# Separate slots and groups of 6, 6 and 4 K-tiles in the first stage, and norms in halves of 1024 columns, in a two-block transformer kernel

## The reference, cut to what matters

```python
mod = c_act @ w_ada[l] + b_ada[l]
sh_m, sc_m, gt_m, sh_f, sc_f, gt_f = jnp.split(mod[:, None, :], N_MOD, axis=-1)
h = rmsnorm(x, pre_mix_norm[l]) * (1.0 + sc_m) + sh_m
proj = h @ w_in[l]
...
y = jnp.concatenate([o_hg, o_gdn], axis=-1) @ w_out[l]
x = x + gt_m * rmsnorm(y, post_mix_norm[l])
h = rmsnorm(x, pre_ffn_norm[l]) * (1.0 + sc_f) + sh_f
y = jnp.square(jax.nn.relu(h @ w_ff1[l])) @ w_ff2[l]
x = x + gt_f * rmsnorm(y, post_ffn_norm[l])
```

## Time and profile before

| | |
|---|---|
| median of 3 runs | 3014.21 us (3013.37 to 3015.81) |
| the profiled execution | 3014.85 us, its span 3013.1 us |
| PE busy | 2709.6 us, 90% of the span |
| weight loads of PE (overlapping) | 2199.4 us, 73% |
| DVE, ACT, POOL busy | 1822.8 us (60%), 1225.0 us (41%), 64.0 us (2%) |
| read from HBM | 556.28 MB, 186 GB/s over the span |

### The profile page before, as it was taken

The page is one execution under the profiler, slowest core; times in us unless marked ns, Lnnn a source line. Parts: engine busy times, 40 slices in busy tenths (PEclk is TensorE's granted clock), DMA queues, the critical chain, the costliest instruction groups (busy, mean ns, idle before and its releaser), DMA issues.

```text
span 3013.1 us, 32417 instructions
## 1 busy us (share of the span) xinstructions
PE 2709.6 (90%) x12554; PEld 2199.4 (73%) x12554; DVE 1822.8 (60%) x2185; ACT 1225.0 (41%) x1523; POOL 64.0 (2%) x90
## 2 busy tenths in 40 slices
PE   4799997587889999999988999998989999999985
PEld 2368885586668888888866877776768888788874
DVE  7669776765675555555674456667455555646454
ACT  2033444442444443444434444443544434444342
POOL 1000000000000000000001000000000000000000
PEclk8899999898989999999999999998999999999998
DMA  9977994034655555555663534444445556555451
GB/s 343 300 204 262 332 324 157 28 138 163 219 196 196 182 192 183 184 192 188 219 249 130 192 123 140 151 144 162 144 143 180 195 175 201 167 196 180 152 171 69
DMA packets 154463, 562.29 MB, mean 187 GB/s; under 512 B 9704, under 2 KB 18023, under 8 KB 150256
## 3 DMA queue, kind: packets, MB, share of 16 engines
q1 hardware_dynamic: 149968, 540.05, 52.8%
q0 software_dynamic: 4208, 20.32, 1.9%
q10 hardware_dynamic: 176, 0.40, 0.0%
HBM read 556.28 MB, written 4.46 MB: 186 GB/s over the span
## 4 chain that ended last, share of the span: by engine, by line
PE 69%; DVE 14%; issue 9%; ACT 5%; DMA 2%; POOL 1%; DVEq 0%; ACTq 0%; SPq 0%; POOLq 0%
PE banks L405 21%; PE banks L407 20%; PE banks L406 20%; ACT weights_high L352 3%; PE banks L640 2%; DVE weights_low L363 2%; PE banks L463 1%; DMA raw_weights<-in_w_in 1%; DVE x_rows L448 1%; DMA raw_weights<-in_w_ada 1%; DVE modulation L2296 1%; DVE mod_in L726 1%; DVE proj L1030 1%; DVE lhs_low L476 1%; POOL small L550 1%
## 5 line engine op out<-in xcount | busy, mean ns | idle before, releaser
L363 DVE TENSOR_TENSOR weights_low<-raw_weights,weights_high 128x1024 fp32r<-128x1024 f32 (+2 forms) x846 | 991.0, 1179 | 934.9 <-ACT weights_high L352 931.4
L352 ACT ACTIVATE weights_high<-raw_weights 128x1024 fp32r<-128x1024 f32 (+2 forms) x846 | 858.8, 1021 | 1026.9 <-PE banks L407 976.6
L405 PE MATMUL banks<-weights_high,lhs_high 128*128 128x512 f32 (+1 forms) x2208 | 875.9, 397 | 34.3 <-DVE weights_low L363 18.4
L407 PE MATMUL banks<-weights_high,lhs_low 128*128 128x512 f32 (+1 forms) x2208 | 860.2, 390 | 0.0
L406 PE MATMUL banks<-weights_low,lhs_high 128*128 128x512 f32 (+1 forms) x2208 | 859.7, 389 | 0.0
L405 PEld LDWEIGHTS banks<-weights_high,lhs_high 128*128 128x128 f32 x2208 | 416.7, 189 | 128.3 <-DVE weights_low L363 19.8
L407 PEld LDWEIGHTS banks<-weights_high,lhs_low 128*128 128x128 f32 x2208 | 416.6, 189 | 86.5
L406 PEld LDWEIGHTS banks<-weights_low,lhs_high 128*128 128x128 f32 x2208 | 417.2, 189 | 79.3 <-issue 0.2
L405 PE MATMUL banks<-weights_high,hid_high 128*128 128x512 f32 x856 | 336.6, 393 | 19.1 <-DVE hid_low L2273 9.8
L407 PE MATMUL banks<-weights_high,hid_low 128*128 128x512 f32 x856 | 334.9, 391 | 0.0
L406 PE MATMUL banks<-weights_low,hid_high 128*128 128x512 f32 x856 | 334.7, 391 | 0.0
(11 more groups left out here) (392 smaller groups left out, 2112.3 us busy)
## 6 DMA issues: line engine op xcount, KB each, us to landing
raw_weights<-in_w_ff SPq DMA_DIRECT2D x128, 1024.0 KB, 5.0
raw_weights<-in_w_in SPq DMA_DIRECT2D x96, 1024.0 KB, 5.5
raw_weights<-in_w_ada SPq DMA_DIRECT2D x84, 1024.0 KB, 5.7
raw_weights<-in_w_up SPq DMA_DIRECT2D x80, 1024.0 KB, 4.9
raw_weights<-in_w_down SPq DMA_DIRECT2D x42, 1024.0 KB, 5.1
raw_weights<-in_w_out SPq DMA_DIRECT2D x32, 1024.0 KB, 5.0
raw_weights<-in_w_ada SPq DMA_DIRECT2D x16, 768.0 KB, 6.3
raw_weights<-in_w_in SPq DMA_DIRECT2D x16, 768.0 KB, 6.9
```

What stands on the lines that cost most here:

```text
L352: act.activation(WHI[:, u % SPN, 0:c.width], RAW[:, n % RAWN, k % 2, 0:c.width], ACT.Copy).then_inc(S("high_made"), 1)
L363: dve.tensor_tensor(WLO[:, u % SPN, 0:c.width], RAW[:, n % RAWN, k % 2, 0:c.width], WHI[:, u % SPN, 0:c.width].bitcast(F32), ALU.subtract) ...
L405: nc.tensor.matmul(o, x, hi, start=(k == 0), stop=False)
L407: mm = nc.tensor.matmul(o, y, hi, start=False, stop=(k == c.kn - 1))
```

## The change

It has five parts.

- **First stage.** The K-tiles of `w_in` get four slots of their own (`FIRST_W`, laid over `weights_high` and `weights_low`), with waits of their own (`first_in`, `first_used`). The groups are 6, 6 and 4. A table (`FIRST_AFTER`) says behind which `w_ada` load SP issues each K-tile. The rows `x` are loaded after the second load rather than the sixth. POOL's loads of masks and small rows follow the second group of gates rather than the third.
- **Norms in halves.** `norm_ffn1`, `norm_in2` and `norm_ffn2` are built by one function (`norm_steps`). Columns 0 to 1023 are normed, transposed and split ahead of unit 0; columns 1024 to 2047 are normed by DVE behind unit 3, and transposed by PE ahead of unit 4. Square sums are taken in pieces, those of a chunk's first half while the next chunk runs, and one mean and power serves both row tiles where that can be.
- **Modulation rows made ahead.** The sum of row 2 stands inside the `w_out` product (ahead of unit 11 of its first chunk), that of row 3 in the last `w_ff2` chunk (ahead of unit 1), both in banks 4 to 7. The `w_out` result is taken out by a new kind of step, "post": ACT squares the bank, DVE multiplies it by the gate row. The last loads of `w_ada` stand earlier, four of them after each pair of units of the second `w_ff1` chunk, and none in the last `w_ff2` chunk.
- **Waits of the transposed rows.** PE no longer waits for the last subtraction before unit 0, but ahead of each second unit for the pair of K-tiles that it uses (`tile_waits`); so also for `mix1`, `norm_mem` and `norm_cross`.
- **The end.** The last norm is written in four pieces, each stored by SP as 512 KB, in place of two stores of 1 MB by POOL. In the `w_in_2` product the narrow product stands six units later, and the distance rows three a unit rather than two.

```diff
+        (FIRST_W,) = region(("first_weights", [128, 4, 2 * UW], F32))
-        GROUPS = [(0, 6), (6, 4), (10, 4), (14, 2)]
+        GROUPS = [(0, 6), (6, 6), (12, 4)]
+        FIRST_AFTER = {MODS[0][13]: [0], MODS[0][15]: [1], MODS[2][3]: [10], MODS[2][5]: [11, 12], MODS[2][7]: [13, 14, 15]}
+        for k in range(8):
+            FIRST_AFTER[MODS[1][2 * k + 1]] = [k + 2]
...
+                for k in FIRST_AFTER.get(x, []):
+                    if k >= 4:
+                        sp.wait_ge(S("first_used"), k - 3)
+                    sp.dma_start(first_tile(k), a["w_in"][128 * k:128 * k + 128, 4 * UW:4 * UW + FIRST_COLS]).then_inc(
+                        S(f"first_in{k % 4}"), 16)
...
+            for b, t, h, w, count, (sem, value), col in out_banks(c, i, ("post",)):
+                dve.wait_ge(sem, value)
+                dve.wait_ge(S("squares_summed"), SQUARES_BEFORE["post_mix"] + b + 4 * (col // UW) + 1)
+                dve.tensor_tensor(Y[:, t, col + 512 * h:col + 512 * h + w], PS[:, b, 0:w],
+                                  MOD[:, 0, col + 512 * h:col + 512 * h + w], ALU.mult).then_inc(S(f"bank_free{b}"), 1)
...
+            def wait(k):
+                def f(pe):
+                    pe.wait_ge(S("round_free"), round_of[name] + k // 2 + 1)
+                return f
...
+            fns = [wait(k) if k % 2 == 0 else None for k in range(KT)]
...
+        def dve_residual(dve, link, name, rows):
+
+            dve_rstd_joint(dve, link, name)
+            for t in range(TT):
+                for h in range(2):
+                    cs = slice(UW * h, UW * h + UW)
+                    dve.scalar_tensor_tensor(out=X[:, t, cs], in0=rows[:, t, cs], scalar=rstd(name, t), in1=X[:, t, cs],
+                                             op0=ALU.mult, op1=ALU.add).then_inc(S("rows_ready"), 1)
...
+            def dve_first(dve):
+                link = Chain(dve)
+                residual(dve, link)
+                dve_norm_half(dve, link, NORM_OF[name], 0, w, shift)
+                dve_split(dve, name, LH2, LL2, 8)
+
+            def dve_half(dve):
+                dve_norm_half(dve, Chain(dve), NORM_OF[name], 1, w, shift)
+
+            def dve_second(dve):
+                dve_split(dve, name, LH2, LL2, 8, first=8)
...
+            return dict(pe=tile_waits(name, (0, pe_first), (4, pe_second)), act=[act_first, None, None, None, act_second],
+                        dve=[dve_first, dve_half, None, None, dve_second])
...
+        def sp_end(sp):
+            for n in range(4):
+                t, h = divmod(n, 2)
+                sp.wait_ge(S("h_ready"), 11 + n)
+                sp.dma_start(out[128 * t:128 * t + 128, UW * h:UW * h + UW], Y[:, t, UW * h:UW * h + UW]).then_inc(
+                    S("out_written"), 16)
```

More of the change, by code:

```diff
@@ L746, in dve_first @@
             dve.wait_ge(S("columns_ready"), 1)
-            dve.wait_ge(S("cond_ready"), 1)
-            mods = [[x for x in FIRST_LOADS if x[0] == "mod" and x[1] == q] for q in range(4)]
-            for n, x in enumerate(mods[0]):
+            dve.wait_ge(S("start_mapped"), 1)
+            for n, x in enumerate(MODS[0]):
                 sums(x)
@@ L1144, in pe_mix1 @@
             mm.then_inc(S("gdn_out"), 1)
-            pe_split(pe, "mix1", P, ready=(S("mix1_ready"), 1))
+            pe_split(pe, "mix1", P, ready=(S("mix1_ready"), 1), wait=False)
         def act_mix1(act):
@@ L1456, in pool_norm_ffn1, with pe_mod_sum @@
             pool_rstd(pool, "pre_ffn")
-        def act_norm_ffn1(act):
-            act_squares(act, "post_mix", Y)
-            act_squares(act, "pre_ffn", X)
-            act_split(act, "norm_ffn1", LH2)
-        def pe_mod_sum(pe, name, row, steps):
+        def pe_mod_sum(pe, row, steps):
             pe.wait_ge(S("ada_used"), steps)
             for b in range(4):
-                pe.wait_ge(S(f"bank_free{b}"), AT[name]["done"][b])
-                mm = nc.tensor.matmul(PS[:, b, :], ONES, MOD[:, row, 512 * b:512 * b + 512], start=True, stop=True)
+                mm = nc.tensor.matmul(PS[:, 4 + b, :], ONES, MOD[:, row, 512 * b:512 * b + 512], start=True, stop=True)
@@ L1469, in pe_mod_sum, with norm_steps, pe_first, pe_second @@
             mm.then_inc(S("mod_summed"), 1)
-        def pe_norm_ffn1(pe):
-            pe_mod_sum(pe, "norm_ffn1", 2, ADA_IN + KT)
-            pe_split(pe, "norm_ffn1", Y, ready=(S("h_ready"), 2))
-        def dve_norm_ffn1(dve):
-            link = Chain(dve)
-            for b in range(4):
-                dve.wait_ge(S(f"bank_free{b}"), AT["norm_ffn1"]["done"][b])
-            dve_rows_ready(dve)
+        def norm_steps(name, squares, residual, w, shift=None, more=()):
+            h0 = H_BEFORE[name]
+            def pe_first(pe):
+                pe_split(pe, name, Y, 8, ready=(S("h_ready"), h0 + 1), wait=False)
+            def pe_second(pe):
+                pe_split(pe, name, Y, 8, ready=(S("h_ready"), h0 + 2), first=8, wait=False)
+            def act_first(act):
+                squares(act)
+                act_split(act, name, LH2, 8)
+            def act_second(act):
+                act_split(act, name, LH2, 8, first=8)
+            def dve_first(dve):
[7 more added lines that the diff above has]
+                dve_split(dve, name, LH2, LL2, 8, first=8)
+                for f in more:
+                    f(dve)
+            return dict(pe=tile_waits(name, (0, pe_first), (4, pe_second)), act=[act_first, None, None, None, act_second],
+                        dve=[dve_first, dve_half, None, None, dve_second])
@@ L1480, in dve_norm_ffn1, with pe_mod2, dve_mod2 @@
+        H_BEFORE = dict(norm_ffn1=0, norm_in2=2, norm_ffn2=8)
+        NORM_OF = dict(norm_ffn1="pre_ffn", norm_in2="mix_in", norm_ffn2="ffn2_in")
+        def pe_mod2(pe):
+            pe_mod_sum(pe, 2, ADA_IN + KT)
+        def dve_mod2(dve):
             dve.wait_ge(S("vecs_in"), 32)
-            dve.wait_ge(S("x2_in"), 16)
             dve.tensor_tensor(MOD[:, 0, :], MOD[:, 0, :], VEC[:, :], ALU.mult)
             dve.wait_ge(S("mod_summed"), 3)
-            link(dve.scalar_tensor_tensor(out=MOD[:, 2, :], in0=bank_cols(0, 4), scalar=1.0, in1=VEC2, op0=ALU.add,
-                                          op1=ALU.mult))
@@ L2092, in pe_norm_mem @@
         def pe_norm_mem(pe):
-            pe_split(pe, "norm_mem", MEMR, ready=(S("h_ready"), 6))
+            pe_split(pe, "norm_mem", MEMR, ready=(S("h_ready"), 6), wait=False)
         def dve_norm_mem(dve):
@@ L2106, in pe_norm_cross @@
         def pe_norm_cross(pe):
-            pe_split(pe, "norm_cross", Y, ready=(S("h_ready"), 8))
+            pe_split(pe, "norm_cross", Y, ready=(S("h_ready"), 8), wait=False)
         def dve_norm_cross(dve):
@@ L2409, in _ @@
             stream(sp_chunk, sp)
+            sp_end(sp)
         @block.scalar
```

337 lines of the change are left out of this document (198 added, 139 removed).

## The result

The changed kernel takes 2971.15 us (median of 4 runs, 2969.34 to 2973.16). In the same session the kernel before took 3015.01 us. The ratio is 0.9853 with a 95% interval of 0.9838 to 0.9867: faster by 43.9 us, where 29 less were forecast (2986). The forecast was right in its sign and too small in its size. The profiled execution took 2972.81 us, 42.0 less than that of before.

What follows compares the result with a forecast made beforehand. PE was taken as the bound, so only its pauses and the end could be won: -7.5 - 4.8 - 11.3 - 7.8 - 3.3 - 3.4 + 9.1 = -29.0 from 3014.85, forecast 2986, range 2971 to 3001.

Steps and rivals of the forecast that it cites:

- the two sums inside full products and the take-out of `w_out`: Added cost: modulation-row sums now inside full products, 7.0 us, and bank 0 freed later in `w_out`, 0.6.
- Rival (c): First stage comes near its transfers and norms lose less to the clock: 2977, down to 2971; chance 0.13.
- Rival (e): Products start sooner but PE's clock stays low after pauses: 35 us more, 3050; chance 0.03.
- the 108 to 117 asked for: Sign of being right in the first stage: K-tile 6 starts between 108 and 117 us.
- Rival (d): Cover of the norms' second halves too thin, 3 to 4 us in each of three norms: 2997; chance 0.10.
- The first stage: First stage, up to the last K-tile: 7.5 us less, bounds 13 less and 1 more.
- the 5 us for small rows: First stage: some 5 us lost to POOL's small rows before the third group's sums are ready.
- the 5 us behind K-tile 10: First stage: 5 us in which SP stands behind K-tile 10 for the slot of K-tile 6.
- The end: After the last product: last piece written earlier and a smaller store by SP, 3.4 us less.
- The waits: Waits before unit 0 of `mix1`, `norm_mem` and `norm_cross` go: 1.6 us each, 4.8 in all.
- 1.5 for each start at the low clock: In each of three halved norms, first units run at low clock: 1.5 us taken off the gain.
- the give-back: In each halved norm, 3.4 us off the gain: 1.9 for the second 16 transposes, 1.5 for low clock.

Runs made afterwards that it cites:

- e4: Changed kernel with the old groups of 6, 4, 4 and 2 K-tiles, own slots kept; last K-tile ends at 166.7 us (164.1 in the changed kernel).
- e5: Kernel before with the new groups of 6, 6 and 4 K-tiles, still in shared slots; ratio 0.9987 to the kernel before.
- e6: Changed kernel with POOL's masks and small rows behind the third group of gates, as before; last K-tile ends at 165.6 us.
- e3: Kernel before with its two 1 MB final stores issued by SP instead of POOL; ratio 0.9982 to the kernel before.
- e1: Changed kernel with its four 512 KB final stores issued by POOL instead of SP; ratio 0.9883 to the kernel before.
- e7: Changed kernel with one wait for all subtractions in `mix1`, `norm_mem` and `norm_cross`, as before; ratio 0.9860 to the kernel before.
- e8: Changed kernel with `cross_in`'s squares and norm moved later in the `w_ckv` product; ratio 0.9835 to the kernel before.
- e12: Changed kernel with `cross_in`'s squares and norm later, `clear_y` later, second gates behind one `w_ada` load; 2963.0 us, ratio 0.9817 to the kernel before.

## Why the prediction was right or wrong

**Right.** That work inside the full products isn't where the gain lies, but PE's pauses and the end; the two sums inside full products and the take-out of `w_out`, 7.6 forecast and 7.7 measured; `norm_ffn1` within 1.1. Rival (c), "-13 there and -3 elsewhere", was nearest, at 2977. Rival (e) fell: the stretch of 33.58 us for K-tiles 6 to 11, behind a pause, is no longer than the 33.9 forecast.

**Signs of being wrong that came.** K-tile 6 started at 106.83, ahead of the 108 to 117 asked for. And PE stood for `weights_low` at unit 7 of `w_ff1`, where my sum had 0.8 us of slack. Rival (d) had named this, at 3 to 4 us in each of three norms; it was 1.55 in one.

**The first stage, 8.9 us of the 13 missed.** The step that failed is "at 305, the rate of the next 80, it is 112. I take 108". The rate rose with the slots to 339 (336 in e4, 305 in e5), over 60 to 103 us even to 374, and the 37.9 MB were in by about 103, near the 104 that 365 GB/s give. With that K-tile 6 started 5.7 us before the 112.5 forecast. Then three smaller ones: the 5 us for small rows and the 5 us behind K-tile 10 fell together (e6); the third group's sums were ready at 139.6, not 148; and the last four K-tiles took 20.87, not 22.7. The 12.26 in that sum was a row at low clock: behind its pause of 1.15 the granted clock was 0.60 over 4 us, while in e3, with the same code, it was 1.00 and the 24 matmuls took 10.57. In the changed kernel the clock held over that pause. So the gain lay outside my own bound of 13. Timeline of PE of e3:

```profile
167.61 10.57 PE L640 MATMUL banks<-raw_weights,x_turned 128*128 128x512 f32 x24 [1.15 <-ACT x_turned L678]
```

As for the Trainium skill's limit near 358 GB/s (DMA: Bandwidth & Descriptors, "Where 436 GB/s comes from"): by that rule the stage would have gained about 9.5. The stage moved 370 GB/s over its first 60 us and 374 over the next 43, so the measurement speaks against a limit there; the gain of 16.4 says less, as it holds the three smaller terms too.

**The end, 6.0 us.** "SP's store is then 512 KB rather than 1 MB, and the earlier ones are gone by then: 1.5". I priced the store by its length and not by who issues it, and so put at nothing what e1 and e3 show to be 5.6 to 6.0 us. The rest was right: with POOL's stores (e1) the end shrinks from 20.7 to 17.3, by the 3.4 forecast. The trace of before had the answer: the last write ends at 3001.9, the landing takes 4.9, and the span ends at 3013.1, 6 us later, with no transfer in it.

**The waits, sum near by luck, places wrong.** Forecast 1.6 each, 4.8 in all; measured a gain of 2.0, a loss of 1.5 and a gain of 3.5, 4.0 in all. At `norm_mem` I left out what the start would run into: the sentence "The first pairs are long subtracted" looked at PE's own operands and not at ACT and DVE, which owe `cross_in` at that moment. At `norm_cross` I left out the clock.

**The clock in the norms.** I took 1.5 for each start at the low clock as new. But the kernel before paid it too, on its transposes. Busy time by stretch of the kernel before, ahead of unit 0 of `norm_ffn1` and behind it:

```profile
839.00:841.00 2.00, 1.99 (x10) 1.99 (x11) 1.97 (x2) 0.60 (x1) 0.00 (x0) 0.50 0.00 0
841.00:843.00 2.00, 2.00 (x11) 2.00 (x11) 2.00 (x4) 1.47 (x3) 0.57 (x1) 0.50 0.07 12
...
847.00:849.00 2.00, 1.96 (x9) 1.62 (x10) 1.21 (x1) 0.10 (x1) 0.00 (x0) 1.00 0.03 8
```

In both kernels some 4 us at 0.50 (1.2 GHz) follow the long pause (814 to 818 in the changed one), then 1.00 (2.4 GHz). It is paid once in either, so most of the 1.5 wasn't new, and `norm_in2` and `norm_ffn2` gained 1.5 and 1.7 more than forecast. In `norm_in2` the sum can be followed: unit 0 starts 18.6 us after the product's end, as forecast, so what didn't come is the give-back. In `norm_ffn1` it was eaten up: 1.55 at units 7 and 8, and 0.9 more of waiting for `hid_rows` at the end of the chunk (3.09 rather than 2.16).

**Code that the change leaves alone, +2.3.** Two chunks took 1.6 us longer each, at a lower clock; one stretch took 1 us less. The first stands behind the last `hid_low` wait. The changed kernel, then e1, whose code is the same up to the last stores:

```profile
1503.00:1509.00 6.00, 6.00 (x20) 4.75 (x21) 1.68 (x2) 1.06 (x1) 0.00 (x0) 0.72 0.81 287
```

```profile
1505.00:1511.00 6.00, 6.00 (x27) 4.96 (x28) 2.21 (x2) 1.32 (x2) 0.00 (x0) 1.00 0.73 254
```

This one differs between executions: of the eleven traces of the changed kernel and its variants, five have the slow chunk (49.6 us) and six the fast (48.0). The second chunk stands behind a pause of 1.57 at 2159.23 and differs by kernel: it takes 24.4 us in all eight traces that have the stand of 3.3 at `norm_mem` some 80 us earlier, and 22.8 in the six that haven't (before, e3, e5, e7, e8, e12). So these 1.6 us may be a part of what that stand costs; how it would reach so far isn't shown.

## What to carry to other kernels

When a change starts an engine sooner, price not only the pause that it removes but the next thing which that engine needs, and who is busy then; here the earlier start at `norm_mem` was lost on work of ACT and DVE that could as well stand four to nine units later. Price a transfer rate by what held it down: if the change removes the stalls in which a rate was measured, take that rate as the floor and not as a middle; here it went from 305 to 339. And follow the last store to the end of the span in the trace, since the queue that issues it can count for more than its size.
